# Long convolution by even and odd positions at half the frequencies, six GLU tiles moved between its chunks

## The reference, cut to what matters

```python
# hyena branch: depthwise short conv, then a long bidirectional convolution per channel (1024 channels)
x0, x1, v = split(centred_short_conv(hy))
u = x1 * v
y_t = sum_{j>=0} h_fwd[j] u_{t-j} + sum_{j>=1} h_bwd[j] u_{t+j} + bias * u_t
branch_hy = (x0 * y) @ w_hy_out
# S5 branch: GLU of the readout
glu_v, glu_g = split(gelu(y_ssm) @ w_glu)
branch_s5 = glu_v * sigmoid(glu_g)
merged = sigmoid(gate_s5) * branch_s5 + sigmoid(gate_hy) * branch_hy
x = x + gate_mix * (merged @ w_out)
```

## Time and profile before

| | us |
|---|---|
| median of 3 runs | 3038.22 |
| lowest, highest | 3034.26, 3045.84 |
| the profiled execution | 3043.7 |
| its span in the trace | 3041.8 |
| PE busy in the span | 2945.4 (97%) |
| DVE, ACT busy | 1495.8 (49%), 837.3 (28%) |

### The profile page before, as it was taken

One profiled execution on the slowest core, in us unless ns is written; L12 is line 12 of the kernel. 1 busy time (PEld: TensorE's weight loads), 2 busy tenths in 40 slices (PEclk: granted clock), 3 DMA queues, 4 the chain that ended last, 5 costly groups with the idle time before them and its releaser, 6 DMA issues.

```text
span 3041.8 us, 34009 instructions
## 1 busy us (share of the span) xinstructions
PE 2945.4 (97%) x14396; PEld 2421.8 (80%) x14396; DVE 1495.8 (49%) x2058; ACT 837.3 (28%) x1220; POOL 180.4 (6%) x321
## 2 busy tenths in 40 slices
PE   6998999999999999997999999999999999999997
PEld 2587888888888888886878888888888888888886
DVE  5545665876553766665675533322233222332245
ACT  4331443223433332221123222222222222222221
POOL 0000000000222001111000100000000000000000
PEclk9999999999999999999999999999999999999998
DMA  9644332333445446776535633333233333333333
GB/s 404 261 109 101 101 101 99 121 122 128 126 140 175 174 139 246 251 248 233 187 118 180 195 115 96 102 97 97 91 98 102 97 97 93 101 97 97 95 91 112
DMA packets 125816, 428.67 MB, mean 141 GB/s; under 512 B 15984, under 2 KB 20336, under 8 KB 121824
## 3 DMA queue, kind: packets, MB, share of 16 engines
q1 hardware_dynamic: 88432, 305.06, 30.4%
q0 software_dynamic: 31472, 109.89, 11.1%
q10 hardware_dynamic: 5760, 11.54, 1.0%
HBM read 398.21 MB, written 28.18 MB: 140 GB/s over the span
## 4 chain that ended last, share of the span: by engine, by line
PE 89%; DMA 5%; DVE 3%; issue 1%; ACT 1%; POOL 0%; SPq 0%; DVEq 0%
PE ps L1691 26%; PE ps L1693 26%; PE ps L1692 26%; DMA ada_mix<-in_w_ac 2%; PE ps L1661 2%; PE ps L1772 1%; PE ps L1735 1%; PE ps L1708 1%; DMA ada1m<-in_w_ar 1%; DMA hw_raw<-in_w_in 1%; PE ps L1662 1%; PE ps L1599 1%; PE ps L1537 1%; PE ps L1539 1%; PE ps L1538 1%
## 5 line engine op out<-in xcount | busy, mean ns | idle before, releaser
L900 DVE TENSOR_TENSOR hw_lo<-hw_raw,hw_hi 128x1024 fp32r<-128x1024 f32 (+2 forms) x512 | 583.5, 1141 | 1252.1 <-ACT hw_hi L550 1250.5
L550 ACT ACTIVATE hw_hi<-hw_raw 128x1024 fp32r<-128x1024 f32 (+2 forms) x512 | 508.1, 993 | 1639.4 <-DMA hw_raw<-in_w_fi 574.1
L1691 PE MATMUL ps<-h_hi,hw_hi 128*128 128x512 f32 x2272 | 890.7, 392 | 0.1
L1693 PE MATMUL ps<-h_hi,hw_lo 128*128 128x512 f32 x2272 | 885.9, 390 | 0.0
L1692 PE MATMUL ps<-h_lo,hw_hi 128*128 128x512 f32 x2272 | 885.4, 390 | 0.0
L1693 PEld LDWEIGHTS ps<-h_hi,hw_lo 128*128 128x128 f32 x2272 | 427.4, 188 | 89.9
L1691 PEld LDWEIGHTS ps<-h_hi,hw_hi 128*128 128x128 f32 x2272 | 427.8, 188 | 87.9 <-issue 0.7
L1692 PEld LDWEIGHTS ps<-h_lo,hw_hi 128*128 128x128 f32 x2272 | 427.6, 188 | 87.3
L1691 PE MATMUL ps<-act_hi,hw_hi 128*128 128x512 f32 x704 | 274.0, 389 | 0.0
L1693 PE MATMUL ps<-act_hi,hw_lo 128*128 128x512 f32 x704 | 273.9, 389 | 0.0
L1692 PE MATMUL ps<-act_lo,hw_hi 128*128 128x512 f32 x704 | 273.9, 389 | 0.0
(11 more groups left out here) (309 smaller groups left out, 2977.1 us busy)
## 6 DMA issues: line engine op xcount, KB each, us to landing
hw_raw<-in_w_fi SPq DMA_DIRECT2D x176, 512.0 KB, 3.5
hw_raw<-in_w_in SPq DMA_DIRECT2D x128, 512.0 KB, 3.7
ada1m<-in_w_ar POOLq DMA_DIRECT2D x128, 512.0 KB, 4.9
ada_mix<-in_w_ac SPq DMA_DIRECT2D x16, 2048.0 KB, 13.2
hw_raw<-in_w_fo SPq DMA_DIRECT2D x64, 384.0 KB, 3.1
hw_raw<-in_w_fo SPq DMA_DIRECT2D x64, 320.0 KB, 2.8
hw_raw<-in_w_glu SPq DMA_DIRECT2D x32, 512.0 KB, 4.6
hw_raw<-in_w_out SPq DMA_DIRECT2D x32, 512.0 KB, 4.4
```

Of the source, the lines that this page charges most:

```text
L550: act.activation(hw_hi[slot(n)][:, 0:width(n)], hw_raw[slot(n)][:, 0:width(n)], ACT.Copy).then_inc(w_hi, 1)
L900: tt(hw_lo[s][:, 0:w], hw_raw[s][:, 0:w], hw_hi[s][:, 0:w].bitcast(F32), SUB).then_inc(w_lo, 1)
L1691: mm(out, wh(k), xh[:, k0 + k, :], start=first and k == 0, stop=False)
L1693: ins = mm(out, wl(k), xh[:, k0 + k, :], start=False, stop=last and k == nk - 1)
```

## The change

The convolution works with half the frequencies: u at even positions and at odd positions is transformed apart, with 256 frequencies each, and sum and difference of the two are the spectrum at a frequency and at its mirror. The inverse folds in the same way. So `spectrum(q)` is 48 matmuls of 256 columns and `inverse(q)` 48 of 256 columns. DVE's work per pair of frequency tiles grows by a sum and a difference on each side, ACT copies the odd part out of PSUM (`odd_copy`). The bias is added to tap zero of the filter, so `conv_products` is one multiplication. The GLU halves of tiles 0 to 5 (12 halves) run three at a time behind each chunk, in ps[0] and ps[1]; `fill_product` stores value times sigmoid in `part`. The merge then runs tiles of three halves and of one half in turn (ORDER). The gelu and its split move ahead, into units 30 and 31 of the input projection; for that the scan takes 5 and 7 steps per unit and the readout begins two units earlier (P3 10 for 12). The filter's spectrum is loaded by POOL. Rows of `w_ada`: 52 in the merge (64 before) and 44 in the output projection (32 before), and the loads of `xacc` are spread over them.

```diff
-P3 = 12
+P3 = 10
 CW = 256
+N_FILL = 6
+ORDER = [m for j in range(N_FILL) for m in (N_FILL + j, j)] + list(range(2 * N_FILL, KT))
...
+            for r in range(52):
                 ada_in(r)
             pool.wait_ge(w_used, H_OUT)
             pool.dma_start(postab2[:, :, :], postab_d).then_inc(s_pos, 16)
             for g in range(4):
                 pool.dma_start(xacc[:, 4 * g:4 * g + 4, :], x_d[:, 4 * g:4 * g + 4, :]).then_inc(xa_in[g], 16)
-            for r in range(64, 128):
+                for r in range((52, 60, 72, 84)[g], (60, 72, 84, 96)[g]):
+                    ada_in(r)
+            for r in range(96, 128):
                 ada_in(r)
...
+            def fill_gate(m):
+
+                act.wait_ge(w_used, H_MRG + 2 * m + 2)
+                if m:
+                    act.wait_ge(m_free, m)
+                act.activation(sg[:, :], ps[1][:, :], ACT.Sigmoid).then_inc(m_sg, 1)
...
+                even, o = ps[2 + 2 * p][:, :].rearrange("p (s c) -> p s c", s=2), odd[p][:, :, :]
                 dve.wait_ge(pq_ps, n + 1)
+                dve.wait_ge(od_cp, n + 1)
...
+                tt(spec[:, 0, :, :], even, o, ADD)
+                tt(spec[:, 1, :, :], even, o, SUB).then_inc(pq_ev, 1)
                 dve.wait_ge(pq_ev, n + 1)
+                dve.wait_ge(k_in[p], 32 * (q + 1))
+                kr, ki = (kfr[p][:, :, s, :].unsqueeze(2).to_broadcast([P, 2, 2, CW]) for s in range(2))
+                tt(ca[:, :, :, :], spec[:, :, :, :], kr, MUL)
+                link(tt(cb[:, :, :, :], spec[:, :, :, :], ki, MUL))
+                tt(ca[:, :, 0, :], ca[:, :, 0, :], cb[:, :, 1, :], SUB)
+                link(tt(ca[:, :, 1, :], ca[:, :, 1, :], cb[:, :, 0, :], ADD))
+                if n >= 2:
+                    dve.wait_ge(yl, n - 1)
+                tt(yf[p][:, 0, :, :], ca[:, 0, :, :], ca[:, 1, :, :], ADD)
+                tt(yf[p][:, 1, :, :], ca[:, 0, :, :], ca[:, 1, :, :], SUB).then_inc(yv, 1)
...
+            def fill_product(m):
+
                 dve.wait_ge(m_sg, m + 1)
+                tt(part[:, m, :], ps[0][:, :], sg[:, :], MUL).then_inc(m_free, 1)
+
+            for q in range(4):
+                n = H_MRG + 3 * q
+                spectrum_products(2 * q)
                 split_lo(n + 2)
+                if q:
+                    conv_products(2 * q - 2)
+                    conv_products(2 * q - 1)
+                if q < 3:
+                    transposed_u(q + 1)
+                spectrum_lo(2 * q)
+                spectrum_products(2 * q + 1)
+                if q:
+                    conv_lo(2 * q - 2)
+                else:
+                    inverse_table(0)
+                split_lo(n + 3)
+                if q:
+                    conv_lo(2 * q - 1)
+                else:
+                    inverse_table(1)
+                spectrum_lo(2 * q + 1)
+                if q % 2:
+                    fill_product(3 * q // 2)
+                    split_lo(n + 4)
+                    fill_product(3 * q // 2 + 1)
+                else:
+                    split_lo(n + 4)
+                    fill_product(3 * q // 2)
...
-                for e in range(3 if m < 4 else 2 if m < 14 else 0):
+                rows = 4 if m < 2 else 3 if m < 14 else 0
+                for e in range(rows):
                     ada_row(row + e)
...
+            def fill(j):
+
+                m, r = j // 2, j % 2
+                if r == 0:
+                    pe.wait_ge(*((m_free, m) if m else (g_free, 32)))
+                half_unit(H_MRG + j, ps[r][:, :], yg_hi, yg_lo, 0, True, True, each=(ygl, 0) if j == 0 else None)
+
             pe.wait_ge(tb_lo, 2)
+            for q in range(4):
                 spectrum(q)
+                if q == 1:
+                    pe.wait_ge(tb_lo, 4)
+                if q:
+                    inverse(q - 1)
+                if q < 3:
+                    transpose_u(q + 1)
+                for j in range(3 * q, 3 * q + 3):
+                    fill(j)
             inverse(3)
```

More of the change, by code:

```diff
@@ L51 @@
 SCAN_H = 18
-P3 = 12
+P3 = 10
 CW = 256
+N_FILL = 6
+ORDER = [m for j in range(N_FILL) for m in (N_FILL + j, j)] + list(range(2 * N_FILL, KT))
+PARTS = [(m, r) for m in range(N_FILL) for r in range(2)] + [
+    (m, r) for m in ORDER for r in (range(3) if m >= N_FILL else (2,))]
+PLACE = [ORDER.index(m) for m in range(KT)]
 F_IN = 4 * QTILES
@@ L772, in _ @@
             gate_tile(31)
[L774 to L785, removed]
@@ new lines, in _, with merged_hi @@
+            conv_hi(6)
+            conv_hi(7)
+            def merged_hi(i):
+                act.wait_ge(m_sum, i + 1)
+                act.activation(mg_hi[:, ORDER[i], :], S1[i % 2][:, :], ACT.Copy).then_inc(m_hi, 1)
+            n = H_MRG + 2 * N_FILL
+            for i in range(KT):
+                split_hi(n + 2)
+                if i:
+                    merged_hi(i - 1)
+                if ORDER[i] >= N_FILL:
+                    split_hi(n + 3)
+                    act.wait_ge(w_used, n + 2)
+                    act.activation(S0[i % 2][:, :], ps[3 * (ORDER[i] % 2) + 1][:, :], ACT.Sigmoid).then_inc(m_sg, 1)
+                    split_hi(n + 4)
+                n += 3 if ORDER[i] >= N_FILL else 1
@@ new lines, in _, with merge @@
+            for i in range(6, 8):
+                conv_products(i)
+            for i in range(6, 8):
+                conv_lo(i)
+            def merge(i, n):
+                m, a, s = ORDER[i], S0[i % 2], S1[i % 2]
+                if m >= N_FILL:
+                    b = 3 * (m % 2)
+                    dve.wait_ge(m_sg, N_FILL + sum(o >= N_FILL for o in ORDER[:i + 1]))
+                    link(tt(s[:, :], ps[b][:, :], a[:, :], MUL))
+                    v, hy = s, ps[b + 2]
+                else:
+                    v, hy = part[:, m, :], ps[7]
+                dve.wait_ge(gt_in[i % 2], 16 * (i // 2 + 1))
+                tt(s[:, :], v[:, :], gT[i % 2][:, 0, :], MUL)
+                dve.wait_ge(w_used, n)
+                tt(a[:, :], hy[:, :], gT[i % 2][:, 1, :], MUL).then_inc(m_free, 1)
+                dve.wait_ge(m_free, N_FILL + i + 1)
+                tt(s[:, :], s[:, :], a[:, :], ADD).then_inc(m_sum, 1)
@@ new lines, in merged_lo @@
+            def merged_lo(i):
+                dve.wait_ge(m_hi, i + 1)
+                tt(mg_lo[:, ORDER[i], :], S1[i % 2][:, :], mg_hi[:, ORDER[i], :].bitcast(F32), SUB).then_inc(m_lo, 1)
+            n, row = H_MRG + 2 * N_FILL, 0
+            for i in range(KT):
+                full = ORDER[i] >= N_FILL
+                split_lo(n + 2)
+                if i:
+                    merge(i - 1, n)
+                for e in range(2):
+                    ada_row(row + e)
+                if full:
+                    split_lo(n + 3)
+                if i:
+                    merged_lo(i - 1)
+                if full:
+                    for e in range(2, 4):
+                        ada_row(row + e)
+                row += 4 if full else 2
+                if i in (7, 13):
+                    ada_mod((i - 7) // 6, ps[6])
+                if full:
+                    split_lo(n + 4)
+                n += 3 if full else 1
@@ L1389, in _ @@
+            merge(KT - 1, n)
             merged_lo(KT - 1)
@@ L1866, in _ @@
                     ada_columns(5, ps[0])
-                each = (m_lo, 0) if m == 0 else None
+                each = (m_lo, PLACE) if m == 0 else None
                 half_unit(n, out, mg_hi, mg_lo, 0, True, False, each=each)
```

467 lines of the change are left out of this document (215 added, 252 removed).

## The result

The kernel before takes 3037.3 us (median of 8 runs, 3027.8 to 3045.8), the changed one 3060.5 us (median of 8, 3054.7 to 3069.6). The ratio is 1.0077, with a 95% interval of 1.0058 to 1.0097: slower by 0.6 to 1.0%, 23 us. The prediction said 3058. The profiled execution of the changed kernel has a span of 3060.8 us, at a mean granted clock of 0.982.

A forecast was written before the change was run, and what follows sets the result against it. Matmuls bound 1000 to 1366 us; in the output projection's start, to 1436, late weight low parts behind VectorE's wait for a third row. Terms -0.8 - 4.2 + 1.8 + 22.6 = +19.4 on median 3038.2 gave 3058, range 3030 to 3080.

The forecast's parts named there:

- start: Everything before the convolution: its first matmul comes 0.8 us earlier, at 999.0, bounds -2 and +4.
- convolution and 12 halves: Convolution with its GLU halves: 43.5 us of matmuls saved, mostly lost to waits and clock; 162.8 against 167.0, -4.2.
- merge: Merge with 36 halves: 198.2 of work plus 3 for VectorE's tight list, against 199.4; +1.8.
- output projection: Output projection with 44 rows for 32: third row's landing seen in twelve tiles; 222.5 against 199.9, +22.6, bounds -3 and +36.
- clock term: Convolution: each of four fill waits of 7 to 9 us loses 3.2 us of matmul; 12.8, bounds 0 and 13.
- Just enough; I add 3 (bounds 0 and 8): Merge, two tiles: VectorE's list of 18.4 and row waits of about 3 fit TensorE's 21.8; 3 us allowed for the stage.
- a start that moves by more than 5 us: Sign of being wrong, at the convolution's first matmul: it would move by more than 5 us.
- cycle of a tile with three rows: Output projection: 13.8 us from residual to residual, bounds 11.9 and 14.8, where TensorE needs 10.9; twelve such tiles 165.6.
- The third row lands quickly: Rival, output projection: landing 3.9 us each time, cycle 11.9, stage -3 to 0; 3035, no change; chance 0.22.
- The fill waits are hidden: Rival, convolution: product reached before the border, four waits and their clock go, -45, 3013; 0.13, simple halving included.
- VectorE paces everything: Rival, whole kernel: merge +8, output cycle 14.8 (+15), start delayed by 4; 3083; chance 0.13.
- The arithmetic halves and nothing else: Rival, convolution: -43.5 of matmuls and -6.3 of waits, 2988; chance 2 in 100.

The follow-up runs named there:

- experiment 2: The changed kernel with the gate's sigmoid and the fill product moved earlier in ScalarE's and VectorE's lists of the convolution; 3037.2 us, ratio to before 1.0005.
- experiment 5: The changed kernel with the convolution reordered: inverse product and transpositions between two GLU halves, ScalarE's and VectorE's lists following; 3020.0 us, ratio to before 0.9954.
- experiment 4: The changed kernel with four row buffers instead of two for w_ada in both merge and output projection; 3013.7 us, ratio to before 0.9921.
- experiment 1: The changed kernel with four row buffers instead of two for w_ada in the output projection only; 3016.2 us, ratio to before 0.9932.
- experiment 3: The changed kernel with the halved convolution but no GLU halves in it; merge and output projection arranged as before; 3025.1 us, ratio to before 0.9963.

## Why the prediction was right

By its own terms, each side the mean of that kernel's two profiles (the convolution ends at its last inverse matmul and is counted with 12 halves of 5.44 on the side of before, as the prediction did):

| term | predicted | before | after | measured |
|---|---|---|---|---|
| start | -0.8 | 997.3 | 994.2 | -3, within one execution's variation |
| convolution and 12 halves | -4.2 | 97.6 + 65.3 = 162.9 | 158.9 | -4.0 |
| merge | +1.8 | 270.8 - 65.3 = 205.5 | 212.9 | +7.4 |
| output projection | +22.6 | 198.9 | 224.3 | +25.4 |
| sum | +19.4 | | | +26; medians of the runs: +23 |

**Convolution: right in the mechanism and the waits; the -4.2 is luck.** Predicted were four waits of 9.3, 8.3, 6.7 and 8.4 us, 32.7 together, each for the fill product; the trace has 8.82, 8.30, 7.77 and 8.02, 32.9 together. For chunk 1 TensorE was to go on 26.4 us after its forward matmuls had begun: 1054.09 less 1027.67 is 26.4. Experiments 2 and 5 show that it is the order. The clock term was too high: predicted 12.8, with a clock near 0.5 behind each wait, and experiment 5, which has the same matmuls without the waits, puts it at 8.1 (158.96 - 36.4 of waits = 122.6; 117.92 - 3.4 = 114.5), with 0.58 to 0.70. The work was estimated 2.8 too high as well (117.3), while two short waits of 3.5 together were left out. So the stage was to be 162.8 and is 159.0. The difference to before comes out all the same, because the side of before was too long too.

One cut of mine was wrong. I ended the convolution of the kernel before at 1101.5, but its last inverse matmul ends at 1096.75; the first 4.8 us of the merge were in it. A wait of 1.3 us at 1100.92, for the gelu's low part, lies in that stretch; the earlier trace rows doesn't have it, and it belongs to the merge. The cut cancels in the sum of before, but it made 48 halves of 5.44 and three column sums of 1.2 look like the whole merge. With the right cut and the table's side of before, the prediction's own stages, 162.8 and 201.2, are -0.1 and -4.3; measured are -4.0 and +7.4.

**Merge: the step that failed is the size of one term.** "Just enough; I add 3 (bounds 0 and 8)." It was 12: 200.4 of work, by experiment 4 (my 198.2 had the column sums too cheap), and 212.2 measured, of which 7.4 are waits of TensorE and the rest clock (0.98). The place was right: in front of each of the four splits that TensorE waits for, VectorE had stood 2.0 to 3.7 us for a row. Of its 36.8 us of waits for rows, 7.4 reach TensorE, and I had not counted the clock that such waits cost, as I did in the other two stages. That all 12 are the rows is not shown, since experiment 1 lost only 2.5 us with the same two buffers.

**Output projection: right, mechanism and size.** The cycle of a tile with three rows was to be 13.8; it is 13.6 and 13.9 in the two profiles. The stage was to be 222.5; it is 222.6 and 226.0. Its parts were off by little each way: the landing is 4.9 in the mean and not about 5.8, and VectorE waits three times in the stage for a weight's high part (7.6 us together), which the cycle of 8.0 without the landing didn't have. The Trainium skill (DMA: Bandwidth & Descriptors, section Anatomy of one DMA) makes it an estimate of 5.6 for three transfers that share the engines, and the cycle 13.6. The trace has 5.5 in the tile shown, which agrees, 4.9 in the mean, and 13.6 for the cycle; between that and my 13.8 these profiles don't decide.

**The rivals.** *The third row lands quickly* would have had residuals 11.9 apart; they are 13.6. *The fill waits are hidden* is not how this kernel is, but experiment 5 makes it true by order alone; its price was put at 45 and measures 41. *VectorE paces everything* is out: in experiments 1 and 5 the same VectorE work fits in stages 39 and 41 us shorter. (Its price was 3 us too high: a cycle of 14.8 for 13.8 is 12 over twelve tiles, not 15.) *The arithmetic halves and nothing else* (2988) is out by experiment 3: 90.4 us for a stage whose matmuls take 60.

**The sum, and the start.** 3058 against 3060.5 is closer than its terms. In the first profile the stages and the start miss by -7.2 (start, 991.8 for 999.0), -3.8 (convolution), +11.0 (merge) and +0.1 us, and cancel. One of my signs of being wrong, a start that moves by more than 5 us, was met there, with 8.0; in the second pair of profiles the start moves by 1.8 the other way, so it doesn't speak against the mechanisms.

What stays open: why the merge with two row buffers takes 203 us in some kernels and 213 in others, and what delays the early part of an execution: the first matmul of the recurrence's input (`ps<-u,m_in`) starts anywhere from 291.3 to 297.7 us in these profiles.

## What to carry to other kernels

Halving the matmuls of this stage moved its bound to the engine that prepares their operands. Matmuls of another stage can fill the room, but whoever puts them there must ask, at each PSUM bank that is used again, which instruction frees it and how deep that instruction stands in its engine's list. Here its place cost 41 us, and putting other matmuls at the border got all of it back. A wait that goes gives its clock back too (experiments 1 and 5); in experiment 2 the waits halved and the clock hardly came back. Count a prefetch's buffers against what its consumer takes in one piece: a third row with two buffers shows its whole landing in every tile (three buffers weren't tried). The Trainium skill (Trainium Kernel Development and Optimization, section Best Practices) names double-buffering, to overlap DMA with compute; with three rows to a tile two buffers cost 39 us in one stage, and with four TensorE waited 1.5 us.

## What the runs showed of the hardware

Eight microseconds of idle TensorE cost about two more behind them: four waits of 8 us took 8.1 us of matmul through the granted clock (124.65 us busy against 116.51 in experiment 5). Shorter waits cost more for their length: four of 1.4 to 5.4 us, 15.0 together, took 6.6 (123.07 in experiment 2), and twelve of 0.4 to 4.2 us in the output projection, 29.2 together, 11.5 (193.4 against 181.9 in experiment 1), where the four of 8, 32.9 together, took 8.1. Four rows on their way at once beside the weights did not make the weights late: DMA share 0.70 instead of 0.61, 251 GB/s instead of 207, and TensorE waited 1.5 us instead of 29.2. Executions of the same code differ by up to 8 us at the start of the convolution (999.8, 994.8 and 991.7), which is a third of the effect here; a difference between two single profiles counts only where a wait or an instruction's place goes with it.
